# A decoder layer's prompt attention: sparse groups reordered by query tile, values multiplied the other way round, compressed branch once per group, stage ends without store waits

## Chip, cores and metric

One Trainium2 chip, one of its NeuronCores. The metric is the device time of one execution in microseconds (us); lower is better. TensorE (PE) multiplies, VectorE (DVE) and ScalarE (ACT) do elementwise work and reductions, GpSimd (POOL) elementwise work too, SyncE (SP) issues nearly all DMAs. Each engine runs its own instruction stream in order and waits on semaphores.

## What is computed

One layer of a decoder for 512 prompt tokens and 8 sequences of 4 new tokens with 1024 cached ones, in fp32. Cut to what matters here:

```python
proj = rmsnorm(x) @ w_in                      # q, kv, gates, diff q/k/v, merge gates ga, gb
# (A) sparse attention: 16 heads in 4 groups of 4 heads; a group shares its keys and values
s_c = q @ kc.T * scale + bias                 # compressed: 32 blocks of the prompt
s_s = q @ k_sel.T * scale + bias              # selected (for the prompt: all causal keys)
s_w = q @ k_win.T * scale + bias              # sliding window (causal, 512 keys)
o_a = g0*softmax(s_c)@vc + g1*softmax(s_s)@v_sel + g2*softmax(s_w)@v_win
# (B) differential attention: 8 heads, (softmax(s1) - lam*softmax(s2)) @ v, rmsnorm per head
o = sigmoid(ga)*o_a + sigmoid(gb)*o_b
h = x + o @ w_o ;  y = h + relu(rmsnorm(h) @ w_up)**2 @ w_down
```

Outputs are y and the new cache rows.

## The kernel before

The program is five stages, one after the other on all engines: `project` (pj_ tiles), `compress` (cm_), `prompt_attention` (pa_), `decode_attention` (de_) and `finish` (fi_). A stage ends with a barrier over all engines, then its semaphores are cleared and a second barrier stands (`Space.clear`, L95 and L96). At the end of `project`, `compress` and `prompt_attention` SP first waits until the stage's last stores have landed (L418, L826, L1337).

`prompt_attention` walks a list of **units**. First 32 units of the differential heads (`Head`, 8 heads by 4 query tiles t of 128 queries). Then 4 groups of 24 units (`Branch`): for each half hp (two heads of the group) and each query tile t the three branches br 0 (compressed, 32 keys), 1 (selected) and 2 (window), the last two with 128(t+1) keys. A unit does, for its two heads:

- `scores` (PE, L1417): one matmul per head, contraction over 64 rows, the two heads in the two halves of the rows; into bank pair n%2 of `pa_ps_s`.
- `score` (DVE, L1519): adds the bias, writes `pa_sc`, and finds the row maximum (`pa_nmax`).
- `exps` (ACT, L1464): exponential in place, with row sums.
- `turn` (PE, L1430): transposes the probabilities by tiles of 128 into `pa_ps_t`, one bank per head; there are **two banks** for all transposes, used in turn (`TURN_ORDER`, `place`).
- `copy` (ACT L1479 for the first head, DVE L1534 for the second): the turned tiles to `pa_p_t`.
- `values` (PE, L1441): out = P V; the turned probabilities (128 x 128) are the weights and the values (128 x 64) move. fp32 matmuls are two instructions in the trace, transposes one.
- per query tile, after its third unit, `scale_branches` (DVE L1557 to L1559) and `combine_branches` (DVE L1566, L1569), which weigh and add the three branches; POOL then merges with the differential part (L1371, L1372).

Two units are one turn of each engine's loop (j = 0, 2, ...). Transposes and copies are for units j-4 and j-3 (`LAG = 4`). `FILL` says at which j the next head's or group's queries and keys are transposed (`fill`, L1407; copied by ACT L1471 or DVE L1527): a group's at 4 and 2 units before its first unit and 2 after.

SP loads groups 0 and 1 at the start (`load_group`, 12 DMAs each) and group g+2 when all of g is combined. Once the heads are done it also loads for the decode stage: the selected pages, the 8 window pages (`win_load` into `shared.ahead.win`, 256 KB each) and one key page of its first pair of sequences.

In `compress`, DVE at the start fills constants, lays out input half 1 (`lay_out(1)`, L928), then makes the low parts of half 0 (`low_parts`, L951), which TensorE's first large matmul (L1058) waits for.

## Time and profile before

| | |
|---|---|
| time, median of 3 runs | 1687.33 us (1680.7 to 1696.27) |
| profiled execution: time | 1688.51 us |
| profiled execution: span of the instructions | 1686.7 us |
| project / compress / prompt attention / decode attention / finish, by the first instruction of each on PE | 7.5 / 405.2 / 631.1 / 955.3 / 1220 us |
| PE, DVE, ACT busy over the span | 95%, 48%, 34% |
| mean granted TensorE clock | 0.967 of 2.4 GHz |

The span is divided by the stages' starts. PE's busy share is of records whose ends are modelled, so a PE that is always busy isn't a PE at its peak; the distance between starts tells more. The granted clock is 1.00 (2.4 GHz) or 0.50 (1.2 GHz) at any instant.

### The profile page before, as it was taken

The page shows a single profiled execution, that of the slowest core. Times are in us where ns is not written, and L with a number is a line of the kernel's source. Part 1 is how long each engine was busy: PE and PEld are TensorE (multiplying, and loading weights), DVE is VectorE, ACT ScalarE, POOL GpSimd, SP SyncE. Part 2 cuts the span into 40 slices and gives each one's busy share as a digit, 9 for nine tenths or more (in the row PEclk, how much of TensorE's full clock was granted, in tenths as well). Part 3 has the DMA queues.
Part 4 walks back from the last instruction along what each step waited for, and adds up shares of the span by engine and source line. Part 5 has one row for each costly group of instructions (what it writes and reads, how often), then busy time and mean ns, then how long its engine had stood idle before and what let it go on. Part 6 is the DMA issues. An engine that isn't in the chain of part 4 may idle for free. (4 is left out here: it accounts for less than half of the span.)

```text
span 1686.7 us, 31658 instructions
## 1 busy us (share of the span) xinstructions
PE 1603.4 (95%) x12648; PEld 1327.3 (79%) x12648; DVE 801.3 (48%) x1835; ACT 574.1 (34%) x1197; POOL 173.0 (10%) x269
## 2 busy tenths in 40 slices
PE   8999999998999988899899889999899999999998
PEld 5788888875888875667777676666687999999998
DVE  3776633215443418866666545454364442234322
ACT  5323211323322327756555333233333331123210
POOL 1000000000630000084212000000000000000000
PEclk9999999999999998989989799999999999999999
DMA  6445477434631307454121399999742334333421
GB/s 194 155 158 171 164 257 289 153 91 97 188 106 28 107 10 203 99 184 130 34 89 33 112 391 366 368 345 330 279 151 91 125 100 125 100 125 99 125 75 54
DMA packets 185433, 265.67 MB, mean 158 GB/s; under 512 B 35805, under 2 KB 117149, under 8 KB 185190
## 3 DMA queue, kind: packets, MB, share of 16 engines
q1 hardware_dynamic: 174930, 227.31, 41.3%
q0 software_dynamic: 6016, 25.34, 5.0%
q10 hardware_dynamic: 4372, 11.49, 1.8%
q8 instruction: 73, 1.20, 0.3%
q14 instruction: 42, 0.34, 0.1%
HBM read 241.01 MB, written 42.60 MB: 168 GB/s over the span
## 5 line engine op out<-in xcount | busy, mean ns | idle before, releaser
L641 PE MATMUL pj_ps<-all_hi,pj_xh 128*128 128x512 f32 x480 | 192.6, 401 | 0.0
L643 PE MATMUL pj_ps<-all_hi,pj_xl 128*128 128x512 f32 x480 | 190.6, 397 | 0.0
L642 PE MATMUL pj_ps<-all_lo,pj_xh 128*128 128x512 f32 x480 | 190.5, 397 | 0.0
L1464 ACT ACTIVATE pa_sc<-pa_sc,pa_nmax 128x32 f32<-128x32 f32 (+4 forms) x256 | 125.9, 493 | 112.4 <-DVE pa_nmax L1519 111.9
L2763 PE MATMUL fi_ps<-fi_fl,fi_wh 128*128 128x272 f32 x512 | 148.6, 290 | 0.0
L2764 PE MATMUL fi_ps<-fi_th,fi_wl 128*128 128x272 f32 x512 | 148.3, 290 | 0.0
L2762 PE MATMUL fi_ps<-fi_th,fi_wh 128*128 128x272 f32 x512 | 147.6, 288 | 0.7 <-DVE fi_tl L2541 0.7
L2762 PE MATMUL fi_ps<-fi_fh,fi_wh 128*128 128x272 f32 x512 | 147.8, 289 | 0.0
L2764 PE MATMUL fi_ps<-fi_fh,fi_wl 128*128 128x272 f32 x512 | 147.7, 288 | 0.0
L2763 PE MATMUL fi_ps<-fi_tl,fi_wh 128*128 128x272 f32 x512 | 147.2, 287 | 0.0
L2110 ACT ACTIVATE de_slot<-de_ps_t 128x512 f32<-128x512 f32 (+5 forms) x124 | 62.8, 513 | 172.7 <-PE de_ps_t L1944 84.4
L2220 DVE COPY de_slot<-de_ps_t 128x512 f32<-128x512 f32 (+4 forms) x112 | 68.7, 622 | 102.5 <-PE de_ps_t L1944 58.9
L641 PEld LDWEIGHTS pj_ps<-all_hi,pj_xh 128*128 128x128 f32 x480 | 90.7, 189 | 24.6 <-issue 3.4
L643 PEld LDWEIGHTS pj_ps<-all_hi,pj_xl 128*128 128x128 f32 x480 | 90.6, 189 | 21.9
L642 PEld LDWEIGHTS pj_ps<-all_lo,pj_xh 128*128 128x128 f32 x480 | 90.7, 189 | 21.0
L1058 PE MATMUL cm_ph<-cm_xh,all_hi 128*128 128x512 f32 x256 | 103.1, 403 | 2.5 <-DVE cm_xl L951 2.5
L2465 ACT ACTIVATE fi_wh<-all_big 128x2048 fp32r<-128x2048 f32 x30 | 57.3, 1909 | 138.5 <-PE fi_ps L2764 138.5
L1059 PE MATMUL cm_ph<-cm_xl,all_hi 128*128 128x512 f32 x256 | 102.3, 400 | 0.0
L1060 PE MATMUL cm_ph<-cm_xh,all_lo 128*128 128x512 f32 x256 | 102.2, 399 | 0.0
L1430 PE MATMUL pa_ps_t<-all_ident,pa_sc 128*128 128x128 f32 (+1 forms) x464 | 78.4, 288 | 24.1 <-ACT pa_q_t L1471 10.6
L2762 PEld LDWEIGHTS fi_ps<-fi_th,fi_wh 128*128 128x128 f32 x512 | 96.4, 188 | 0.8 <-DVE fi_tl L2541 0.8
L2762 PEld LDWEIGHTS fi_ps<-fi_fh,fi_wh 128*128 128x128 f32 x512 | 96.5, 189 | 0.0
(347 smaller groups left out, 3164.9 us busy)
## 6 DMA issues: line engine op xcount, KB each, us to landing
de_dv<-in_cache_diff SPq DMA_DIRECT2D x64, 512.0 KB, 9.8
all_big<-in_w_in SPq DMA_DIRECT2D x14, 2048.0 KB, 10.6
de_dk<-in_cache_diff SPq DMA_DIRECT2D x48, 512.0 KB, 9.0
all_big<-in_cache_nsa SPq DMA_DIRECT2D x64, 256.0 KB, 6.5
all_big<-in_w_up SPq DMA_DIRECT2D x16, 1024.0 KB, 5.5
all_big<-in_w_down SPq DMA_DIRECT2D x16, 1024.0 KB, 5.7
all_win<-in_cache_win SPq DMA_DIRECT2D x32, 256.0 KB, 7.7
all_dk<-in_cache_diff SPq DMA_DIRECT2D x16, 512.0 KB, 8.5
```

The lines of the kernel that those rows point to most:

```text
L641: pe.matmul(ps[:, t, :], xh[:, k, xk], wh[:, u, k, :], start=k == 0, stop=False)
L642: pe.matmul(ps[:, t, :], xh[:, k, xk], wl[:, u, k, :], start=False, stop=False)
L643: return pe.matmul(ps[:, t, :], xl[:, k, xk], wh[:, u, k, :], start=False, stop=k == KT - 1)
L1058: pe.matmul(o, w1h[k][:, kt, col], mh, start=first, stop=False)
L1059: pe.matmul(o, w1h[k][:, kt, col], ml, start=False, stop=False)
L1060: ins = pe.matmul(o, w1l[k][:, kt, col], mh, start=False, stop=last)
L1430: ins = pe.transpose(bank[0:r, P * k:P * (k + 1)], sc[:, x.n % 6, a, P * k:P * k + r], ident[:])
L1464: nc.scalar.activation(tile, tile, ACT.Exp, scale=-1.0, bias=nmax[:, x.n % 6, a:a + 1], accum_out=x.sums[a]).then_inc(probs, 1)
L2220: ins = nc.vector.tensor_copy(slot[rows, g % 4, cols], ps_t[rows, g % 4, cols])
L2762: pe.matmul(o, hi[:, k, :], a_hi[:, k, tok], start=k == 0, stop=False)
L2763: pe.matmul(o, hi[:, k, :], a_lo[:, k, tok], start=False, stop=False)
L2764: return pe.matmul(o, lo[:, k, :], a_hi[:, k, tok], start=False, stop=k == n_k - 1)
```

## The change

In `prompt_attention`, for the sparse groups only (the heads' units stay):

- A group has 16 units in place of 24 (`NG = 2*QT*2`): selected and window of a query tile, so that one turn of the loop is one query tile.
- The two branches' values are multiplied together (`wide_values`): the values (128 x 64) are the weights, one branch in columns 0 to 63 of the array and one in 64 to 127, and the turned probabilities of both heads (256 columns) move. The result is transposed: ACT copies it (`wide_copy`), PE turns it back (`turn_back`, 2 transposes), DVE combines.
- The compressed branch is done once per group for all 4 heads and 4 tiles: scores (`cs`, 2 fills of 8 matmuls), one maximum, subtraction and exponential over 128 x 512, 4 transposes (`cp`), 4 matmuls with a block-diagonal value matrix (`co`), sums and products on DVE. The next group's transposes and these are put at -10, -8, -6, -4, -2, +4 and +6 units from a group's first unit.
- ACT copies three of four turned blocks (selected of both heads, window of the first), wide results and all key fills; DVE one of four. The order within a turn of ACT's and DVE's loops changes.
- Scratch room is lent from the decode stage's window buffer: 6 of its 8 pages are now loaded in the last group, 2 at the start of the decode stage.
- SP's waits for landed stores go from the ends of the three stages to where the rows are read; in `compress`, `lay_out(1)` comes after the first `low_parts`.

The core of the diff (buffers, semaphores and load lists left out; new PE and DVE parts in full where they are short):

```diff
@@ compress, vector engine
             fill()
-            lay_out(1)
...
                 low_parts(v)
                 if v == 0:
+                    lay_out(1)
                     split()
@@ project / compress / prompt_attention, end of sync engine (each stage alike)
-            for k in range(2):
-                sp.wait_ge(stored[k], 16 * (N_PAIRS + 1))
+            shared.cmp_level = 16 * (N_PAIRS + 1)
@@ prompt_attention
-        NH, NG = DHEADS * QT, 2 * QT * 3
+        NH, NG = DHEADS * QT, 2 * QT * 2
-            FILL[b - 4] = [("q", x, 0), ("k", x, 0)]
-            FILL[b - 2] = [("k", x, 1), ("c", x, 0)]
-            FILL[b + 2] = [("q", x, 1)]
+            for n, more in ((-10, [("q", x, 0)]), (-8, [("k", x, 0)]), (-6, [("k", x, 1), ("c", x, 0)]), (-4, [("q", x, 1)]),
+                            (-2, [("cs", x, 0), ("cs", x, 1)]), (4, [("cp", x, 0)]), (6, [("co", x, 0), ("co", x, 1)])):
+                FILL[b + n] = FILL.get(b + n, []) + more
+        MAX_CMP, EXP_CMP, SUM_CMP = ({first_of(g) + n: g for g in range(GROUPS)} for n in (0, 2, 4))
@@ tensor engine
+            def wide_values(x):
+                pe.wait_ge(combined, x.tile - 1)
+                stand()
+                for unit in (UNITS[x.n - 1], x):
+                    for entry in unit.turns:
+                        pe.wait_ge(*of(entry))
+                        stand()
+                for k in range(x.t + 1):
+                    for unit in (UNITS[x.n - 1], x):
+                        ins = pe.matmul(unit.wide_part, unit.values[k], p_t[:, unit.br, :, P * k:P * (k + 1)],
+                                        start=k == 0, stop=k == x.t)
+                ins.then_inc(wide_done, 1)
+            def turn_back(x):
+                pe.wait_ge(wide_copied, x.m + 1)
+                stand()
+                for a in range(2):
+                    ins = pe.transpose(x.wide[:, a, :], o_t[:, a, :], ident[:])
+                ins.then_inc(valued, 1)
...
                 for x in FILL.get(j, []):
                     fill(x)
+                if NH <= j - LAG - 2 < N:
+                    wide_values(UNITS[j - LAG - 1])
                 for n in (j - LAG, j - LAG + 1):
...
+                if NH <= j - LAG - 2 < N:
+                    turn_back(UNITS[j - LAG - 1])
@@ scalar engine, a turn of the loop within the groups
+                    for x in fills:
+                        fill_copy(x)
+                    if j < N:
+                        exps(UNITS[j])
+                    if NH <= j - LAG - 2:
+                        wide_copy(UNITS[j - LAG - 1])
+                    if j in EXP_CMP:
+                        act.wait_ge(cmp_ready, EXP_CMP[j] + 1)
+                        nc.scalar.activation(cmp_p, cmp_p, ACT.Exp).then_inc(cmp_probs, 1)
+                    for n in (j - LAG, j - LAG + 1):
+                        if n < N:
+                            copy(UNITS[n])
+                    if j < N:
+                        exps(UNITS[j + 1])
@@ vector engine, a turn of the loop within the groups, after score(UNITS[j]), cs / co and score(UNITS[j + 1])
+                    scale_branches(UNITS[j - LAG + 1])
+                    copy(UNITS[j - LAG + 1])
+                if NH <= j - LAG - 2 < N:
+                    combine_branches(UNITS[j - LAG - 1])
+                if j in MAX_CMP:
+                    cmp_most(MAX_CMP[j])
+                if j in SUM_CMP:
+                    cmp_sums(SUM_CMP[j])
@@ combine_branches: 128 x 256 product, then two 128 x 128 sums, in place of 128 x 384 product and reduction
@@ decode_attention, sync engine
             load_new(0)
+            for n in range(6, 8):
+                win_page(sp, d, shared, 0, *divmod(n, WINDOW // P))
...
+            for u in range(2):
+                sp.wait_ge(shared.oa_out[u], 32 * (GROUPS // 2))
```

`cmp_most` is a reduction of 128 x 512 to 128 x 16, a small clamp and a 128 x 512 subtraction; `cmp_sums` a 128 x 512 reduction, a clamp, a reciprocal and 4 small products; `cmp_scores` (cs) adds the bias to 128 x 256 of PSUM, twice; `cmp_outputs` (co) multiplies 128 x 512 of PSUM by coefficients, twice.

## Rows read from the trace of the kernel before

**Rows 1.** The page: busy time of the engines, and the granted clock in 40 slices.
```profile
PE 1603.4 (95%) x12648; PEld 1327.3 (79%) x12648; DVE 801.3 (48%) x1835; ACT 574.1 (34%) x1197; POOL 173.0 (10%) x269
...
PEclk9999999999999998989989799999999999999999
```

**Rows 2.** Stretches: start and end, length, busy per engine, granted clock, DMA share, GB/s.
```profile
762.04:822.01 59.97, 55.06 (x403) 43.91 (x402) 40.53 (x166) 35.09 (x126) 22.19 (x42) 0.91 0.28 82
704.00:882.00 178.00, 162.92 (x1164) 127.38 (x1164) 119.63 (x488) 99.56 (x372) 70.84 (x130) 0.90 0.33 104
882.00:952.00 70.00, 62.84 (x473) 51.21 (x472) 44.65 (x177) 34.30 (x128) 15.36 (x30) 0.92 0.08 24
955.00:1218.00 263.00, 247.31 (x3584) 178.74 (x3584) 122.68 (x345) 84.32 (x165) 11.14 (x20) 0.95 0.96 348
783.30:790.10 6.80, 6.80 (x24) 4.09 (x24) 3.56 (x10) 2.09 (x8) 6.25 (x14) 0.50 0.95 275
796.90:800.40 3.50, 3.32 (x32) 2.98 (x31) 1.63 (x10) 2.56 (x10) 2.06 (x3) 1.00 0.03 11
```

**Rows 3.** Order of time on all engines, one turn of the loop in group 1.
```profile
797.67 0.40 ACT L1464 ACTIVATE pa_sc<-pa_sc,pa_nmax 128x128 f32<-128x128 f32 x1 [1.86 <-DVE pa_nmax L1519]
799.08 1.09 PE L1430 MATMUL pa_ps_t<-all_ident,pa_sc 128*128 128x128 f32 x8 [0.18 <-ACT pa_p_t L1479]
800.01 1.90 PE L1441 MATMUL pa_ps_o<-pa_vs,pa_p_t 128*128 128x64 f32 x16
801.84 0.49 PE L1417 MATMUL pa_ps_s<-pa_keys,pa_q_t 64*128 64x256 f32 x2
```

**Rows 4.** Who waited for whom, 704 to 946 us: total us, times, longest.
```profile
ACT pa_sc L1464 <- DVE pa_nmax L1519: 98.5, 76, 4.6
DVE pa_p_t L1534 <- PE pa_ps_t L1430: 49.4, 66, 1.9
PE pa_ps_t L1430 <- ACT pa_p_t L1479: 9.5, 17, 1.6
```

**Rows 5.** TensorE in order of time in the decode stage (weights of 32 columns).
```profile
1027.11 1.50 PE L2041 MATMUL de_ps_d<-de_dv,de_slot 128*32 128x512 f32 x12
```

**Rows 6.** Groups in group 1 (762 to 822 us), all forms: busy us, mean ns, idle before.
```profile
L1464 ACT ACTIVATE pa_sc<-pa_sc,pa_nmax 128x32 f32<-128x32 f32 (+4 forms) x49 | 23.4, 478 | 23.9 <-DVE pa_nmax L1519 23.8
L1519 DVE CUSTOM_DVE_ANT_0 pa_sc<-pa_ps_s,pa_strip 128x32 f32<-128x32 f32 (+4 forms) x48 | 16.8, 386 | 5.6 <-PE pa_ps_s L1417 5.5
L1534 DVE COPY pa_p_t<-pa_ps_t 32x128 f32<-32x128 f32 (+4 forms) x25 | 10.6, 425 | 12.6 <-PE pa_ps_t L1430 12.5
L1479 ACT ACTIVATE pa_p_t<-pa_ps_t 32x128 f32<-32x128 f32 (+4 forms) x24 | 8.7, 362 | 0.9 <-PE pa_ps_t L1430 0.8
```

**Rows 7.** The same, by form.
```profile
L1464 ACT ACTIVATE pa_sc<-pa_sc,pa_nmax 128x32 f32<-128x32 f32 x16 | 5.0, 314 | 4.8 <-DVE pa_nmax L1519 4.8
L1464 ACT ACTIVATE pa_sc<-pa_sc,pa_nmax 128x512 f32<-128x512 f32 x9 | 6.4, 713 | 9.8 <-DVE pa_nmax L1519 9.8
L1519 DVE CUSTOM_DVE_ANT_0 pa_sc<-pa_ps_s,pa_strip 128x512 f32<-128x512 f32 x8 | 5.2, 682 | 2.8 <-PE pa_ps_s L1417 2.8
L1479 ACT ACTIVATE pa_p_t<-pa_ps_t 128x256 f32<-128x256 f32 x4 | 1.5, 373 | 0.7 <-PE pa_ps_t L1430 0.5
L1566 DVE TENSOR_TENSOR all_late<-pa_ps_o,pa_coef 128x384 f32<-128x384 f32 x8 | 4.4, 552 | 0.1
L1569 DVE TENSOR_REDUCE pa_oa<-all_late 128x128 f32<-128x384 f32 x8 | 4.8, 595 | 0.3
```

**Rows 8.** SP's own waits at the ends of project, compress and prompt attention.
```profile
SPq L418 <- DMA scratch_gb<-pj_y: 1.7, 1, 1.7
...
SPq L826 <- DMA scratch_vc_p<-cm_out: 1.1, 1, 1.1
...
SPq L1337 <- DMA scratch_oa<-pa_oa: 1.9, 1, 1.9
```

**Rows 9.** TensorE at the start of compress, in order of time.
```profile
410.83 0.47 PE L1058 MATMUL cm_ph<-cm_xh,all_hi 128*128 128x512 f32 x1 [2.45 <-DVE cm_xl L951]
```

More of the change, by code:

```diff
@@ L416, in _ @@
             sp.wait_ge(bias_out, 16 * 3)
-            for k in range(3):
-                sp.wait_ge(stored[k], stores[k])
+            shared.rows_level = stores
         @block.scalar
@@ L1174, in prompt_attention @@
         g_in = [s.sem(f"g_in{u}") for u in range(2)]
+        v_in = [s.sem(f"v_in{u}") for u in range(2)]
         h_in = shared.h_in
@@ L1237, in __init__ @@
-                self.clamp = 3e38 if br else 1e29
+                    self.needs += [("k", DHEADS + g, 0), ("k", DHEADS + g, 1)]
+                first, at = P * (QT - 1 - t), 2 * (1 - g % 2)
+                v = (vs, vw)[br]
+                self.lhs = [q_place(g, hp)[x, P * t:P * (t + 1)] for x in HALF]
+                self.width = P * (t + 1)
+                self.rhs = [keys[x, at + br, 0:self.width] for x in HALF]
+                self.values = [v[:, self.u, k, :] for k in range(t + 1)]
@@ L1238, in __init__ @@
+                self.bias = [strip[:, self.u, 2 * hp + x, first:SEQ] for x in range(2)]
+                self.clamp = 3e38
                 self.sums = [rsum[:, self.m % 8, x, br:br + 1] for x in range(2)]
                 self.turns = [("p", n, x) for x in range(2)]
[L1240 to L1242 removed]
+                self.p_t = [p_t[:, br, x, :] for x in range(2)]
@@ L1305, in load_merge @@
                     sp.dma_start(merge[:, k, :, :], tok(d[name][0:SEQ, HPG * DK * g:HPG * DK * (g + 1)])).then_inc(merge_in, 16)
-            load_group(0, 0)
-            load_group(1, 1)
+            for k in range(2):
+                sp.wait_ge(shared.cmp_stored[k], shared.cmp_level)
+            for g in range(2):
+                load_group(g, g)
+                load_values(g, g)
             for h in range(HEADS_AT_ONCE, DHEADS):
@@ L1327, in _ @@
                 if g + 2 < GROUPS:
+                    sp.wait_ge(turned, TURN["q", DHEADS + g, 1] + 1)
+                    load_group(g + 2, g % 2)
                     sp.wait_ge(combined, NH + 2 * QT * (g + 1))
-                    load_group(g + 2, g % 2)
+                    load_values(g + 2, g % 2)
+                if g + 1 == GROUPS:
+                    sp.wait_ge(copied["dve"], copies[TURN["co", DHEADS + g, 1]])
+                    for n in range(6):
+                        win_page(sp, d, shared, 0, *divmod(n, WINDOW // P))
                 for hp in range(2):
@@ L1473, in copy @@
             def copy(x):
-                r = TURN[x.turns[0]]
-                act.wait_ge(turned, r + 1)
-                if x.free_level > 0:
+                if x.n >= NH:
+                    act.wait_ge(*free_level(x))
+                elif x.free_level > 0:
                     act.wait_ge(valued, x.free_level)
-                rows, w = x.values[0].shape[0], P * len(x.values)
-                nc.scalar.activation(x.p_t[0][0:rows, 0:w], ps_t[0:rows, r % 2, 0:w], ACT.Copy).then_inc(copied["act"], 1)
@@ L1481, in _ @@
-            fill_copy(("q", 0, 0))
-            for j in range(0, N + LAG, 2):
-                if j < N:
-                    exps(UNITS[j])
-                for x in FILL.get(j, []):
-                    if copier_of(x) == "act":
-                        fill_copy(x)
+                for a, entry in enumerate(x.turns):
+                    if copier_of(entry) == "act":
+                        r, w = TURN[entry], P * len(x.values)
+                        act.wait_ge(turned, r + 1)
+                        nc.scalar.activation(x.p_t[a][:, 0:w], ps_t[:, r % 2, 0:w], ACT.Copy).then_inc(copied["act"], 1)
```

257 lines of the change are left out of this document (186 added, 71 removed).

## Prediction

> **What bounds the kernel now.** I read the page first: PE is busy 95% of the span, DVE 48%, ACT 34%, and the granted clock is below full mainly in the middle slices [rows 1]. The reader is to see that PE is the busiest engine throughout. Then the stretches: group 1 of the sparse heads takes 59.97 us from its first scores to the next group's, with PE busy 55.1, DVE 40.5 and ACT 35.1 at a granted clock of 0.91; groups 0 to 2 together take 178 us, group 3 with the stage's tail 70 us [rows 2]. Then one turn of the loop in order of time: PE goes from transposes to values to the next scores with a hole of at most 0.2 us (16 value matmuls from 800.01 to 801.84, 0.114 each), while ACT had stood idle 1.86 us before its exponential [rows 3]. The waits say the same: ACT waits 98.5 us for DVE's maxima and DVE 49.4 us for transposes, but PE only 9.5 us for ACT's copies [rows 4]. So PE's program ends last in most turns.
>
> PE's own work in one group, from start-to-start times: values 192 instructions (2 for each of 80 blocks, 32 compressed) x 0.112 = 21.5; transposes 96 x 0.109 = 10.5 (8 take 1.09 us with the last one's tail [rows 3]); scores, whose 512 columns take about 0.43 us per instruction like the decode stage's 512 columns [rows 5], two heads side by side, 8.5, and compressed 2.0; key and query transposes 17 x 0.11 = 1.9. Sum 44.4 of 60.0 us. The other 15.6 are the clock's dips, changes between kinds of matmul (about 0.2 from start to start instead of 0.11: 801.84 less the start of the sixteenth value matmul [rows 3]) and waits for copies.
>
> **The change on PE.** The weights become 64 columns wide and 256 columns move. Bounded by the nearest row: in the decode stage 12 matmuls with weights of 32 columns and 512 moving ones take 1.50 us [rows 5], three rounds of four at 0.43 and a tail; one behind the other they would take 12 x 0.43 = 5.2. So tiles in different columns of the array run side by side. A block of 128 keys of both branches then costs 2 x 0.213 = 0.43, 20 blocks a group: 8.5 us (one behind the other: 17.1). Transposes of probabilities 80 x 0.109 = 8.7; turning back 16 x 0.109 = 1.7; scores 8.5; cs 32 instructions, which within a fill all use the same half of the rows and are bound by their 128 weight columns as the value matmuls are, 3.5; cp 0.4; co 8 x 0.213 = 1.7; other fills 1.9. Sum 35.0, 9.4 less than now.
>
> **ACT and DVE per group.** ACT: exponentials 23.4 less 5.0 for the compressed ones, 18.4; copies of selected and window, half of them, are 8.7 less 8 x 0.25, three of four 10.1 [rows 6, 7]; 8 wide copies x 0.37, one exponential of 128x512 0.7, fills 3.0: 35. DVE: scores 16.8 less 16 x 0.2, 13.6; one copy of four 4.0; coefficients 5; combining 8 x 0.9 (0.55 for 384 columns, so 0.42 for 256, and two sums of 0.2); compressed work 6.3 (0.6 for a reduction of 384 columns, so 0.7 for 512: cmp_most 1.65, cmp_sums 2.0, cs 0.9, co 1.4, the rest small) [rows 6, 7]: 36. All three engines then have about 35 us of work, so none has slack for the others' latency, and I go by the chain of one turn.
>
> **The chain of a turn.** From PE's start of scores: the previous tile's combination, which waits for the turning back, ends on DVE; the first head's score; on ACT two exponentials, the wide copy and two copies; on PE the last transposes (two banks, so the window's second waits for ACT's second copy) and the turning back. For tile t=3, when tile 1 is turned: scores are ready at 1.25; DVE 0.68 and 0.1 to 2.05; exponentials 2 x 0.71 to 3.5; wide copy 0.37 to 3.85; two copies of 0.37 to 4.6 [rows 7]; two transposes to 4.85, turning back to 5.1, next scores at 5.2. In the same way t=0 takes 4.4, t=1 5.2, t=2 4.75; plus 0.2 each for changes of kind. A half of a group is 20.3, a group 40.7.
>
> Extras per group. ACT's fill copy stands ahead of its exponentials and waits for PE's fill, which stands behind two scores: fills delay the chain by 0.35 (-8), 0.65 (-6), 0.55 (-4). The cs fills hold PE and DVE's second score: 2.8. cmp_most delays the next score by 1.65, its exponential 0.7, cp 0.55. At +6 come cmp_sums' 2.0, co through both banks, the next group's first query fill behind them, ACT's copy of it, and only then ACT's exponentials: 4.4 (2.3 in the last group). Sum 11.65. The clock now falls after turns in which PE waits for fills (783.3 to 790.1 at 0.50 [rows 2]); I expect one such dip a group, after cs, at 1.7 us. A group: 54.0 us against 60.0.
>
> **The sum**, against the profiled execution's 1688.51:
> - Groups 0 to 2: 3 x 54.0 = 162 against 178: -16.
> - Group 3 and tail: 40.7 + 5.2 (its own extras) + 1.7 + 13.4 (three turns without scores, combination, POOL, store) = 61 against 70: -9.
> - Heads: group 0's cs and its second query fill come among them: +3.5, between nothing (hidden) and 5.
> - Stage ends: SP waits 1.7, 1.1 and 1.9 us for landed stores [rows 8], all on the path to the barrier: -4.7. The waits reappear ahead of stores and loads that are not needed soon; between -4.7 and -2 if one of them holds something up. In compress the two layouts of about 1.2 us each ahead of the low parts go; PE idles 2.45 us there before its first large matmul [rows 9]: -2.2. DVE splits weights that much later, behind 12 us of matmuls of half 0.
> - Decode: 512 KB more in a stage with DMA at 0.96 and 348 GB/s [rows 2] is 1.5 us if all of it shows, nothing if none: +1. Its key loads are issued 0.9 us later, within this.
> - SP's queue in the stage: load_group(g+2) moves to before group g and load_values to its end; both have most of a group before they are needed, and the stores of oa behind them wait for the same combination as now. POOL starts at the heads' end as before. Nothing.
>
> Sum: -16 - 9 + 3.5 - 6.9 + 1 = -27.4, so 1661; the median of the runs shown is 1.2 below the profiled execution: **1659 us**, this case's own range 1642 to 1675.
>
> One rule of the Trainium skill speaks against the new mixture of matmuls: "TensorEngine Tiling (Array Packing)", Key Properties, says that changing the tiling mode drains the engine. The trace shows 0.2 us instead of 0.11 at such a change [rows 3]. By a full drain, taken as an estimate at 0.27 us each, some 30 changes of a group would cost 8 us instead of 3, and the time would be 10 us more or so where PE ends last.
>
> **Rivals.**
> - *PE-bound as now* (22%): the engines overlap better than my chain says, and a group keeps its ratio of time to PE work, 60.0/44.4 = 1.35: 47.3 us. For: ACT idles 1.86 us before an exponential today and PE doesn't mind [rows 3]. Against: three equal engines. 4 x 12.7 = 51 saved, heads +3.5, ends -6.9, decode +1: 1634.
> - *The saving is eaten* (14%): the two tiles of weights run one behind the other (+5 of the 8.6, the rest in PE's waits), or the turns at +6 and cs cost double. 59 us a group: about 1680, within 1%.
> - *Slower, by the clock* (10%): fewer and wider matmuls with more waiting between them let the clock fall to 0.50 for much of the stage, as it does from 783.3 to 790.1 [rows 2]. At 1.2 GHz PE's 35 us of a group are 70. Against: 796.9 to 800.4, mostly transposes, was at 1.00 [rows 2, 3]. If about three quarters of PE's work run at the low level a group takes 66: 4 x 6 + 3.5 - 6.9 + 1 = +22, 1710. It decides from about 61 us a group, about half of PE's work at the low level. The Trainium skill, "TensorE: Matmul & The Clock Gate", Part 4: PE-mode transpose, has transposes not count as a busy PE for the clock; by that rule this rival would be likely, since transposes are 10.8 of 35 us after and 10.5 of 44 before. The stretch at 1.00 speaks against the rule here.
> - *It does not do what it says* (4%): the groups stay at 60 us and only the stage ends count, about 1683.
>
> **Chances.** Forecast 50%, PE-bound 22%, eaten or ends alone 18%, slower 10%. A measurement of this kernel tells about 1% from no change, so the bounds are 1670.5 and 1704. A little of the forecast's own range lies above 1670.5: faster 0.70, same 0.20, slower 0.10. The range 1626 to 1690 takes in the PE-bound case and the eaten one, and leaves the slow clock out.
>
> **What would show it.** A group's first scores to the next's: 54 us; tiles 4.6 to 5.4 apart, about 8 to 10 at cs and where co and the next query fill meet. Wide matmuls in pairs that start together, pairs 0.21 apart; if the second starts 0.21 later, the tiles don't run side by side. PE's wait for ACT's copies should grow from 9.5 us to several tens. SP's three waits gone, and PE's first large matmul of compress near 407. Clock in the stage 0.90 or above; near 0.6 the slower rival is right. A group under 50 us means that my chain was too long.

## The result, and the profile after

The changed kernel takes 1663.67 us (median; 1659.93 to 1664.96) against 1687.97 of the kernel before: a ratio of 0.9843, 95% interval 0.9808 to 0.9878. (All ratios here are estimated from the single fast runs and can differ a little from the quotient of the medians, here 0.9856.) Predicted were 1659 us, 1642 to 1675 for the leading case, and a range of 1626 to 1690. The profiled execution took 1662.45 us with a span of 1660.6, against 1688.51 and 1686.7.

Where the 26.1 us of the two spans went, by the first instruction of each stage on PE and the first scores of each group:

| part | before | after | difference | term of the prediction |
|---|---|---|---|---|
| start of `project` (7.5 and 8.9) | | | +1.4 | none |
| end of `project` to start of prompt attention | 230.2 | 225.5 | -4.7 | -1.7 - 1.1 - 2.2 = -5.0 |
| heads | 72.9 | 74.7 | +1.8 | +3.5 |
| groups 0, 1, 2 | 178.0 | 162.5 | -15.5 | -16 |
| group 3, tail, end of the stage | 73.3 | 64.6 | -8.7 | -9 - 1.9 = -10.9 |
| decode attention and finish | 731.4 | 731.0 | -0.4 | +1 |

So the sum held nearly term by term; the last group gave about 2 us less than forecast. The sizes inside the terms did not hold as well, and the reason why a turn takes the time that it takes was not the one that I gave. The first sign is in the groups, which the prediction had all alike. The changed kernel by stretches, from a group's first scores to the next group's (the last to the first decode instruction):

```profile
core 0: us, PE busy (x) PEld busy (x) DVE busy (x) ACT busy (x) POOL busy (x), PEclk, DMA share, GB/s
702.49:750.18 47.69, 40.80 (x276) 27.30 (x276) 35.91 (x130) 31.05 (x100) 28.99 (x52) 0.97 0.32 111
750.18:809.83 59.65, 47.68 (x302) 30.14 (x301) 37.13 (x136) 35.77 (x107) 21.91 (x41) 0.90 0.37 107
809.83:864.97 55.14, 48.16 (x303) 30.90 (x302) 36.28 (x135) 33.26 (x104) 19.27 (x36) 0.87 0.29 86
864.97:929.60 64.63, 50.03 (x324) 31.24 (x323) 41.30 (x154) 36.36 (x111) 16.24 (x32) 0.92 0.17 53
```

The first three answer to the group of [rows 2]: 47.7, 59.7 and 55.1 us against 58 to 60, with a mean of 54.2 where the prediction had 54.0. Since the three lie 12 us apart, that their mean agrees so well is luck in part. DVE (36 to 37 us) and ACT (31 to 36) are as busy as its sums of 36 and 35 said. The granted clock, the column behind POOL, runs from 0.97 to 0.87. A clock of 0.87 over 55.14 us is 14.3 us at the low level (the part at 0.50 is twice what is missing to 1.00); the prediction had one dip of 3.4.

Two heads' and two branches' values, from the timeline of PE:

```profile
738.70 0.38 PE L1525 MATMUL pa_ps_o<-pa_p_t,pa_vs 128*64 128x256 f32 x1
738.70 0.38 PE L1525 MATMUL pa_ps_o<-pa_p_t,pa_vw 128*64 128x256 f32 x1
738.91 0.38 PE L1525 MATMUL pa_ps_o<-pa_p_t,pa_vs 128*64 128x256 f32 x1
738.92 0.38 PE L1525 MATMUL pa_ps_o<-pa_p_t,pa_vw 128*64 128x256 f32 x1
```

The first column is the start. Selected (`pa_vs`) and window (`pa_vw`) start together, the next pair 0.21 us later: a block costs 0.43 us for both, as predicted. By the Trainium skill, "TensorEngine Tiling (Array Packing)", Key Properties, a change of tiling mode drains the engine. A step of that kind shows here: from the last pair of this passage (739.99) to the next transpose (740.31) are 0.32 us instead of the 0.21 of a pair. The trace does not tell that a drain is its cause.

From the waits between 705 and 929 us:

```profile
DVE pa_p_t L1712 <- PE pa_ps_t L1513: 54.7, 29, 4.7
PEld pa_ps_t L1513 <- ACT pa_p_t L1597: 32.8, 33, 3.4
ACT pa_sc L1571 <- DVE pa_nmax L1697: 25.1, 16, 3.5
PE pa_ps_t L1513 <- ACT pa_p_t L1597: 24.1, 28, 3.2
```

PE's wait for ACT's copies grew from 9.5 us to 24.1, ACT's for DVE's maxima fell from 98.5 to 25.1 [rows 4]. Two turns of group 2 show who waits for whom where it is worst. DVE, ACT and PE at the turn that begins at 829.20, where the compressed sums and products stand:

```profile
830.35 0.68 DVE L1665 TENSOR_REDUCE pa_cmp_coef<-all_win 128x16 f32<-128x512 f32 x1
831.06 0.47 DVE L1666 TENSOR_SCALAR pa_cmp_coef<-pa_cmp_coef 128x16 f32<-128x16 f32 x1
831.56 0.25 DVE L1667 RECIPROCAL pa_cmp_coef<-pa_cmp_coef 128x16 f32<-128x16 f32 x1
831.85 1.13 DVE L1670 TENSOR_TENSOR pa_cmp_coef<-pa_cmp_coef,pa_gates 128x4 f32<-128x4 f32 x4
833.19 0.69 DVE L1697 CUSTOM_DVE_ANT_0 pa_sc<-pa_ps_s,pa_strip 128x512 f32<-128x512 f32 x1 [0.21 <-PE pa_ps_t L1463]
...
835.85 0.60 ACT L1580 ACTIVATE pa_q_t<-pa_ps_t 128x512 f32<-128x512 f32 x1 [5.41 <-PE pa_ps_t L1490]
...
835.16 0.66 PE L1490 MATMUL pa_ps_t<-all_ident,pa_q 128*128 128x128 f32 x4 [2.05 <-DVE all_win L1679]
```

DVE makes the sums (830.35 to 832.98) while the scores of the tile wait; then come its two scores and the products; PE's query transposes wait for a bank that the products free, and ACT, in order, waits for those transposes ahead of its exponential. That is the turn at +6 that the prediction priced at 4.4 us extra. Behind both long waits of PE in this group the clock falls: this one is followed by 6.8 us at the low level from 835.8, the wait of 2.65 us that ended at 820.97 by 3.4 us from 822.2. Of the eight falls in the four groups ahead of the stage's tail five come with such a wait, of 2.05 to 3.18 us. The other three (at 747.1, 805.1 and 863.1) come with no wait of PE above 0.32 us in the 7 us before; each comes during the 32 small matmuls of the next group's compressed scores or within 1.4 us of the start of their last. The last of the three, with a line for PE and one for the stretch ahead of the fall (columns as above):

```profile
858.78 3.23 PE L1455 MATMUL pa_ps_t<-pa_kc_t,pa_q_t 64*128 64x32 f32 x32
...
856.00:863.12 7.12, 6.80 (x52) 5.04 (x52) 4.05 (x11) 3.86 (x14) 0.91 (x2) 1.00 0.15 39
```

PE is busy for 6.80 of these 7.12 us, and the clock falls at 863.12 all the same. It is the dip after the compressed scores that the prediction expected; those behind the waits it did not. In e_nocmp below, which has no compressed scores, groups 0, 2 and 3 stay at full clock.

### The profile page after: what moved, and what is told of

Its sections match the earlier page's. It is cut to its first block and busy times, and to the rows that moved or that the text cites. A ratio compares the mean times of both kernels' runs of the same rounds, so it can differ in the third digit from the quotient of the medians.

```text
span 1660.6 us, 30744 instructions
## 1 busy us (share of the span) xinstructions
PE 1564.8 (94%) x12248; PEld 1270.9 (77%) x12248; DVE 789.1 (48%) x1723; ACT 576.7 (35%) x1118; POOL 172.4 (10%) x269
## 3 DMA queue, kind: packets, MB, share of 16 engines
q1 hardware_dynamic: 175506, 227.41, 41.9%
## 5 line engine op out<-in xcount | busy, mean ns | idle before, releaser
L1571 ACT ACTIVATE pa_sc<-pa_sc,pa_nmax 128x128 f32<-128x128 f32 (+3 forms) x192 | 105.5, 552 | 38.5 <-DVE pa_nmax L1697 38.3
L1513 PE MATMUL pa_ps_t<-all_ident,pa_sc 128*128 128x128 f32 x400 | 71.1, 304 | 31.0 <-ACT pa_p_t L1597 24.1
```

What stands on the lines that cost most here:

```text
L1513: ins = pe.transpose(bank[0:r, P * k:P * (k + 1)], sc[:, x.n % 6, a, P * k:P * k + r], ident[:])
L1571: nc.scalar.activation(tile, tile, ACT.Exp, scale=-1.0, bias=nmax[:, x.n % 6, a:a + 1], accum_out=x.sums[a]).then_inc(probs, 1)
```

## The experiments

All are one edit of the changed kernel unless said otherwise. On three of the chips used (those of all runs but e_hide, e_serial, e_nocmp and e_ends), PE had gaps in the compress stage that the first chip does not show, and that stage was about 20 us longer (402 to 646 us against 405 to 628), in the kernel before as well by its median: 1709 to 1711 us instead of 1690. So totals are compared by their ratio to the kernel before on the same chip, and the parts by the length of the prompt attention stage on PE (301.8 us in the changed kernel, 324.2 before). Group 2 by its turns, the distances between the first scores of consecutive query tiles, j counted from the group's first unit:

```
j                      0     2     4     6     8     10    12    14    sum   low clock
changed kernel        4.87  7.59  6.91 10.72  5.71  5.97  5.36  8.00   55.1   14.2
e_hide                4.83  6.29  5.36  8.12  4.51  5.97  5.36  8.02   48.5    4.1
e_nocmp               4.82  5.21  4.93  6.07  4.51  5.97  5.36  5.06   41.9    0
e_serial              5.02  7.71  6.27 10.10  4.63  6.45  6.27  8.38   54.8    3.6
e_late                4.16  6.41  5.36  9.56  4.51  5.97  5.36  8.01   49.3    2.0
e_loads               5.69  5.37  5.39  7.35  4.64  5.97  5.45  8.58   48.4    7.5
e_turns               3.51  6.18  6.39  7.59  4.82  6.12  6.39  9.07   50.1    2.9
```

The last column is the time at the low clock level, in us, by the clock records.

**e_hide: are the compressed passages on the path?**

```diff
@@ vector engine, ahead of the copy of the window block instead of behind the combination
                     scale_branches(UNITS[j - LAG + 1])
+                if j in MAX_CMP:
+                    cmp_most(MAX_CMP[j])
+                if j in SUM_CMP:
+                    cmp_sums(SUM_CMP[j])
+                if NH <= j - LAG < N:
                     copy(UNITS[j - LAG + 1])
```

> The changed kernel with VectorE's compressed maxima (about 1.8 us) and compressed sums (2.8 us) moved to just ahead of its copy of a turned block, where it idles about 2 us a turn for PE's transposes. Chain theory (a turn is a chain over PE, DVE and ACT, and both passages stand in it): about 4 us less a group, 2 in the first, 14 to 16 us in all: 1648 against 1663. PE theory (a group's time follows PE's work, the rest is hidden): within 2 us of the changed kernel, 1662 to 1665.

Measured: 1645.33 us, ratio 0.9733 (0.9707 to 0.9758), 1.1% below the changed kernel; stage 281.8 us, 20.0 shorter. The passages are on the path, and the change that put them there can be improved by two moved calls. The chain theory had 14 to 16 us. DVE at the same place now:

```profile
816.67 0.69 DVE L1665 TENSOR_REDUCE pa_cmp_coef<-all_win 128x16 f32<-128x512 f32 x1
817.39 0.17 DVE L1666 TENSOR_SCALAR pa_cmp_coef<-pa_cmp_coef 128x16 f32<-128x16 f32 x1
817.60 0.25 DVE L1667 RECIPROCAL pa_cmp_coef<-pa_cmp_coef 128x16 f32<-128x16 f32 x1
817.89 0.75 DVE L1670 TENSOR_TENSOR pa_cmp_coef<-pa_cmp_coef,pa_gates 128x4 f32<-128x4 f32 x4
818.67 0.29 DVE L1712 COPY pa_p_t<-pa_ps_t 128x128 f32<-128x128 f32 x1
```

There it used to sit idle for PE's transposes. But the gain is more than the passages: the turn at j=8, which holds none, fell from 5.71 to 4.51, because there the clock is full now. The whole group gained 6.7 us, while 10.1 us less were spent at the low level. Over all four groups that time fell from 39.2 to 15.7 us; at 0.4 us each (b_ends below) some 9 of the 20 us are clock, as an estimate. The gain lies in groups 1, 2 and 3 (6.3, 6.7 and 6.8 us); group 0 gained 0.3.

**e_serial: does PE's work decide?**

```diff
-                for k in range(x.t + 1):
-                    for unit in (UNITS[x.n - 1], x):
+                for unit in (UNITS[x.n - 1], x):
+                    for k in range(x.t + 1):
```

> The changed kernel with all selected blocks multiplied before all window blocks, so that the two column tiles no longer run side by side: 0.43 us more for each of 20 blocks of a group, 8.5 us of PE's work a group. PE theory: it all shows, with the group's ratio of time to work even more, 34 us or above in all, 1698. Chain theory: it shows in the turns where the values end later than DVE's score and ACT's exponentials, and is hidden in the turns that score 512 keys and multiply one block; about 5 to 6 us a group, 1684 to 1688. If the pairs don't really run side by side: no change.

Measured: 1670.13 us, ratio 0.989 (0.986 to 0.9919), stage 305.2 us. Neither expectation, and the trace tells why. Four blocks, PE's timeline (a line with x5 holds five that start 0.2 us apart):

```profile
823.95 1.29 PE L1525 MATMUL pa_ps_o<-pa_p_t,pa_vs 128*64 128x256 f32 x5
824.87 0.43 PE L1525 MATMUL pa_ps_o<-pa_p_t,pa_vw 128*64 128x256 f32 x1
825.08 0.38 PE L1525 MATMUL pa_ps_o<-pa_p_t,pa_vs 128*64 128x256 f32 x1
825.13 0.38 PE L1525 MATMUL pa_ps_o<-pa_p_t,pa_vw 128*64 128x256 f32 x1
...
825.56 1.24 PE L1525 MATMUL pa_ps_o<-pa_p_t,pa_vw 128*64 128x256 f32 x5
```

In the program all eight selected instructions (four blocks of two) stand ahead of all window ones. In the trace the first window one starts at 824.87, when three selected ones have yet to start (the fifth of the line with x5 starts at 824.86). With six of each it starts beside the third (845.18 and 845.19 in another turn), with four or two of each beside the first. So the edit did not cost 8.5 us of PE a group but 0, 0, 2 and 4 instructions of 0.21 us in turns of one to four blocks, 2.6 us a group. And just that shows in the turns: j=10 multiplies three blocks and went from 5.97 to 6.45 (0.48, for 0.43 worked out), j=12 four and from 5.36 to 6.27 (0.91, for 0.86). The same two steps stand at j=10 in groups 0 and 3 and at j=12 in all groups; only the turn at j=10 of group 1 did not grow (7.50 and 7.44). In these turns every bit of PE's time shows, at full clock; my count of hidden values was wrong. That alone does not decide between the theories, since the chain theory also let it show where the values end late; e_late does.

In group 2 as a whole the time did not grow (54.8 against 55.1): the group spent 3.6 us at the low clock instead of 14.2. That the added work is what kept the clock up is not shown. Over the stage 3.4 us were added, of 10 worked out.

**e_nocmp: what do the compressed parts cost?**

```diff
-                            (-2, [("cs", x, 0), ("cs", x, 1)]), (4, [("cp", x, 0)]), (6, [("co", x, 0), ("co", x, 1)])):
+                            ):
-        MAX_CMP, EXP_CMP, SUM_CMP = ({first_of(g) + n: g for g in range(GROUPS)} for n in (0, 2, 4))
+        MAX_CMP, EXP_CMP, SUM_CMP = {}, {}, {}
```

> The changed kernel without the compressed branch's scores, maximum, exponential, transposes, products and sums (its part of the output is left out, the same addition is made of another operand). Chain theory: the extras of a group (cs 2.8, maxima 1.65, exponential 0.7, cp 0.55 and most of the 4.4 where the outputs and the next queries meet) and the dip of the clock go, 10 to 11 us a group and 3.5 among the heads, 1617 to 1622. PE theory: only the 5.6 us of PE's work a group at a ratio of 1.35, 7.6 us a group, 1633. If the compressed work is hidden: above 1650.

Two waits that name the compressed work go or move with it. Measured: 1629.37 us, ratio 0.9634 (0.9606 to 0.9662), stage 262.1 us. The first three groups and one wait:

```profile
696.21:735.56 39.35, 33.79 (x233) 21.40 (x232) 32.65 (x119) 29.66 (x99) 23.33 (x40) 1.00 0.38 135
735.56:789.59 54.03, 39.70 (x258) 24.19 (x258) 31.92 (x122) 34.53 (x106) 26.28 (x51) 0.87 0.30 86
789.59:831.52 41.93, 36.60 (x259) 22.28 (x258) 31.26 (x121) 31.57 (x103) 20.60 (x39) 1.00 0.52 154
```

```profile
PE pa_ps_t L1492 <- DMA pa_kc<-scratch_kc_p: 8.7, 1, 8.7
```

Group 2 takes 41.9 us without them, at full clock, 13.2 less than in the changed kernel, and more than either theory had (10 to 11 and 7.6); the prediction's chain without compressed work is 40.7 + 1.55 (the plain fills) = 42.25. Group 1 is another matter: there PE waits 8.7 us for the load of group 2's keys. SP issues it behind its wait for POOL's squares of the heads. (13.7 us at the low clock follow.) The kernel had got ahead of that load, so the total fell by 34 us and not by the 41 to 46 of the chain theory. The heads are 71.3 us long against 74.7: the compressed scores cost 3.4 there.

**e_ends: the stages' ends**

```diff
@@ end of sync engine in project, compress and prompt_attention
+            for k in range(3):
+                sp.wait_ge(stored[k], stores[k])
@@ compress, vector engine
             fill()
+            lay_out(1)
...
                 if v == 0:
-                    lay_out(1)
                     split()
```

> The changed kernel with SP's three waits for landed stores back at the ends of the stages and input half 1 laid out first again in the compress stage. The sum's term for these was 6.9 us (4.7 + 2.2): 1670.5 against 1663.7. Rival: the waits only moved, and the stages' ends are held by something else too: under 3 us, 1664 to 1666.

Measured: 1671.3 us, ratio 0.9891 (0.9868 to 0.9915), about 8 us more than the changed kernel. On PE the gap between project and compress is 1.7 us longer, compress with its end 3.8 (226.8 against 223.0), the end of prompt attention 2.0 (5.8 against 3.8): 7.5 us where the prediction had 6.9. The term is confirmed by the trace; the two totals' intervals overlap.

**b_ends: the same edits in the kernel before** (without the wait at the end of prompt attention, whose room the stage after it reuses).

> The kernel before with only the waits for landed stores moved away from the ends of project and compress, and input half 1 laid out behind the first low parts (the wait at the end of the prompt attention stays). By the prediction's terms 1.7 + 1.1 + 2.2 = 5.0 us less than before, a ratio of 0.997. If the stages' ends and the start of compress are held by something else: 1.000.

Measured: 1697.65 us, ratio 0.9938 (0.9908 to 0.9969). The 5 us are there: in the trace PE's gaps ahead of compress and of prompt attention are 1.8 and 1.2 us shorter than before (2.53 and 2.75 us), and the first large matmul of compress comes 2.1 us sooner after the stage's first. The profiled execution shows something else beside them. Groups 1 and 2, and behind them group 2 of the kernel before:

```profile
772.59:829.47 56.88, 51.97 (x405) 41.80 (x405) 40.24 (x165) 34.96 (x126) 22.19 (x42) 0.97 0.32 99
829.47:885.49 56.02, 50.53 (x406) 41.28 (x405) 39.97 (x164) 32.04 (x123) 12.56 (x24) 1.00 0.31 92
...
822.01:882.00 59.99, 55.19 (x402) 43.25 (x402) 39.80 (x165) 32.21 (x123) 12.55 (x24) 0.91 0.29 86
```

The program of these groups is that of the kernel before, where they take 60.0 us at 0.91 [rows 2]. Here group 2 has a clock of 1.00 and takes 56.0. That is the price of the clock in this kernel, 4.0 us for 10.2 us at the low level, 0.4 us each; groups 0 and 1, compared in the same way, give 0.35 and 0.45. So how often the clock falls hangs on more than what a group does. (It is another chip, and the groups start at other times; which of the two is the cause is not shown.)

**e_two: the share of the copies.** VectorE copies two of four turned blocks as before the change.

```diff
-            return "act" if kind in ("q", "cp") or early or (kind == "p" and half == 0) or sparse else "dve"
+            return "act" if kind in ("q", "cp") or early or (kind == "p" and half == 0) else "dve"
...
+                    copy(UNITS[j - LAG])
                     scale_branches(UNITS[j - LAG + 1])
```

> The changed kernel with VectorE copying the second head's turned block of both branches (two of four) and ScalarE the first head's, as before the change; DVE's added copy stands after its scores and ahead of the coefficients. If the share of three in four is worth what the chain of a turn says: ACT loses about 0.45 us a turn from its chain, but DVE's copy comes only after four scores, so PE's third transpose waits for it instead: within 8 us of 1663.7 on either side, and slower rather than faster (1664 to 1672). If ACT's time alone decided a turn: 32 x 0.45 = 14 us less, 1649.

Measured: ratio 0.9875 (0.984 to 0.9909), stage 302.3 us against 301.8. No difference that can be told, as the first expectation had it: the share of the copies gives nothing measurable by itself in either direction.

**e_qfirst, e_late, e_best, e_loads: what is late after e_hide.** e_qfirst puts the next group's queries ahead of the compressed products:

```diff
-                FILL[b + n] = FILL.get(b + n, []) + more
+                FILL[b + n] = more + FILL.get(b + n, []) if n == -10 else FILL.get(b + n, []) + more
```

> The kernel with the two compressed passages hidden (1645.3), with the next group's query transposes ahead of the compressed products in the turn where both stand. There ACT idled 5.4 us behind its copy of the queries in the changed kernel. Chain theory: the turn of 8.1 us loses 1.5 to 2.5, in three groups: 5 to 7 us less, 1639. If the queries only trade places with the products: 1645.

Measured: ratio 0.975 (0.9721 to 0.9779), stage 284.6 us against 281.8: a miss. The turn at j=6 fell from 8.12 to 6.82 us in groups 0 and 2, as expected, and rose to 12.27 in group 1. PE's waits from 765 to 800:

```profile
PE pa_ps_t L1490 <- DMA pa_kc<-scratch_kc_p: 3.8, 1, 3.8
```

It is the load of e_nocmp again. e_late moves DVE's combination, and also ACT's square root by one turn:

```diff
@@ vector engine: the combination one turn later, between the two scores
                     score(UNITS[j])
+                if NH <= j - LAG - 4 and j <= N:
+                    combine_branches(UNITS[j - LAG - 3])
...
-                if NH <= j - LAG - 2 < N:
+                if j >= N:
                     combine_branches(UNITS[j - LAG - 1])
```

> The kernel with the two compressed passages hidden (1645.3), with VectorE's combination of a query tile (1.0 to 1.3 us) moved one turn later, between the scores of the next tile's two units, so that DVE scores as soon as PE has the scores; ScalarE's square root one turn later too. Chain theory (DVE's queue ahead of its first score is on the chain): 0.6 to 0.9 us a turn, 28 turns, 17 to 25 us less: 1620 to 1628. PE theory: 1645.

Measured: ratio 0.9759 (0.972 to 0.9799), which e_hide's interval overlaps; stage 280.2 us, 1.6 shorter than e_hide's. By groups: 2.8 us less in group 1, where the square root moved, 1.4 less in group 0, and 0.9 and 0.7 more in groups 2 and 3. In group 2 the turns at j=8, 10 and 12 are the same to the hundredth, 4.51, 5.97 and 5.36: DVE's queue was not on their path. In group 0 it was. There POOL works on the heads' results, DVE's two sums of a combination take 0.77 us each instead of 0.29, and PE waits longer for ACT's copy; the turn at j=8 fell from 5.22 to 4.51, that at j=10 from 6.39 to 5.97. The same transposes at j=8, in e_hide and in e_late:

```profile
726.85 0.93 PE L1513 MATMUL pa_ps_t<-all_ident,pa_sc 128*128 128x128 f32 x6 [1.02 <-ACT pa_p_t L1597]
...
747.62 0.93 PE L1513 MATMUL pa_ps_t<-all_ident,pa_sc 128*128 128x128 f32 x6 [0.31 <-ACT pa_p_t L1597]
```

Two of the turns of group 2 in e_late, j=10 and 12:

```profile
848.52:854.49 5.97, 5.66 (x45) 3.93 (x44) 3.37 (x16) 4.45 (x16) 1.83 (x3) 1.00 0.52 178
854.49:859.85 5.36, 5.04 (x36) 2.82 (x35) 4.25 (x16) 3.80 (x15) 3.78 (x8) 1.00 0.00 0
```

PE is busy for 5.66 of 5.97 us, DVE for 3.4, ACT for 4.5. What is left is PE's wait of 0.31 us for ACT's copy of the first transposed block, since there are two banks. e_late and e_serial agree: a turn without compressed work is bound by PE, as long as POOL does not slow DVE down.

e_best is e_hide, e_qfirst and e_late together.

> The hidden compressed passages, the queries ahead of the compressed products, the combination one turn later and the square root one turn later, together. Apart, the second was eaten by ACT's wait for POOL before the square root (its turn took 12.3 us in group 1) and the third gave nothing where PE is busy all the turn. If that reading is right, the turns with products take about 6.8 us in all groups and group 1 has no such wait: 6 to 9 us less than with the passages hidden alone, a ratio to before of 0.968 to 0.970. If the single results add up as measured: 0.976.

Measured: ratio 0.9761 (0.9725 to 0.9796), stage 279.8 us: the lower expectation is refused, since the turn in group 1 still took 11.15 us. e_loads takes the cause away:

```diff
@@ sync engine
-            sp.wait_ge(o_sq, 1)
-            load_merge(0)
             for g in range(GROUPS):
...
                     load_group(g + 2, g % 2)
+                    if g == 0:
+                        sp.wait_ge(o_sq, 1)
+                        load_merge(0)
                     sp.wait_ge(combined
```

> The combined version with SP's loads of group 2's queries and keys ahead of its wait for POOL's squares, instead of behind it. With the queries first, PE stood 3.8 us in group 1 for such a load, and that turn took 11 to 12 us instead of 6.8 in the other groups. If that load is the cause: group 1 falls from 54.7 us to about 48 to 49, 5 to 6 us in all, a ratio to before of 0.972 to 0.973. If the turn is held by something else (POOL, ACT's square root): 0.976 as before.

Measured: 1664.83 us beside 1709.92 of the kernel before, ratio 0.9735 (0.9696 to 0.9773). The turn in group 1 takes 6.82 us (the others 6.82 to 7.35), and group 1 fell from 54.7 to 49.8 us, some 2 of it by 4.9 us less at the low clock (an estimate, at 0.4 each). The stage is 277.4 us, the shortest of all with the full computation, but 2.4 less than e_best's and not 5 to 6, since group 2 took 1.7 us more, with 7.5 us at the low clock instead of 2.5:

```profile
722.80:768.49 45.69, 41.35 (x277) 27.61 (x276) 36.59 (x127) 30.51 (x97) 26.21 (x47) 0.95 0.43 140
768.49:818.25 49.76, 44.59 (x302) 28.78 (x301) 39.14 (x136) 36.30 (x107) 21.81 (x40) 0.95 0.23 72
818.25:866.69 48.44, 45.81 (x302) 29.27 (x301) 37.73 (x135) 33.88 (x104) 22.39 (x43) 0.92 0.46 133
```

So the cause of the long turn is settled. e_hide and e_loads, 0.9733 and 0.9735, are both faster than the changed kernel; the intervals do not tell them apart, nor from e_best's.

**e_between and e_turns: values between the transposes.**

```diff
@@ tensor engine
-                if NH <= j - LAG - 2 < N:
-                    wide_values(UNITS[j - LAG - 1])
                 for n in (j - LAG, j - LAG + 1):
                     if 0 <= n < N:
                         turn(UNITS[n])
...
+                    if n == j - LAG and NH <= n - 2 < N:
+                        wide_values(UNITS[n - 1])
```

> The kernel with the two compressed passages hidden (1645.3), with the wide value matmuls between the transposes of a turn's two units instead of ahead of both, and ScalarE's wide copy between its copies of the two units. Chain theory (ACT's wide copy of 0.37 us stands between its exponentials and the copies that PE's last transposes wait for): 0.3 to 0.4 us a turn, 10 to 12 us less, 1633 to 1635. If the values end after the exponentials, so that they are the longer branch: within 3 us of 1645.

Measured (on top of e_hide): ratio 0.9857 (0.9824 to 0.9889), stage 303.9 us, 22 longer. A new wait leads ACT's from 720 to 940 us:

```profile
ACT pa_p_t L1597 <- PE pa_ps_o L1525: 40.5, 25, 4.1
```

The room for the turned probabilities is single; ACT may copy the next tile only when the values of the last have been multiplied, which is later now. I had left that wait out. e_turns gives the selected half a second room, on top of e_best:

```diff
+                self.p_all = spare_p if br == 0 and self.m % 2 else p_t[:, br, :, :]
...
-            return (wide_done, x.m) if x.m else (valued, NH)
+            m = x.m - 1 + x.br
+            return (wide_done, m) if m > 0 else (valued, NH)
```

> The previous kernel with the wide values between the transposes of a turn's two units again, but now with a second room for the turned selected probabilities, so that ACT's copies of the first unit need not wait for the values of the tile before (one selected page of the decode stage is loaded at that stage's start instead). If that wait of 40 us in all was what made the order slower, it is gone, and PE no longer idles 0.3 us and more a turn for ACT's copy: 8 to 14 us less than the previous kernel, ratio 0.960 to 0.964, less 0.002 if the late page shows in the decode stage. If the order itself is at fault (values after the first unit's transposes end too late for ACT's wide copy): slower than the previous kernel, 0.975 or more.

Measured: ratio 0.9765 (0.973 to 0.9801), stage 283.4 us against 279.8. The wait of 40 us is gone and the order still does not pay. In the turn at j=12 (6.39 us instead of 5.36) PE meets another:

```profile
859.44 0.33 PE L1516 MATMUL pa_ps_t<-all_ident,pa_sc 128*128 128x128 f32 x1 [0.58 <-ACT pa_q_t L1583]
...
862.66 0.41 PE L1536 MATMUL pa_ps_o<-all_ident,all_late 128*128 128x128 f32 x2 [0.20 <-ACT all_late L1589]
```

The second transpose needs the bank of the query fill, which ACT has yet to copy; and at the end the turning back waits for the wide copy. Values ahead of both transposes cover just these two. By the length of the stage the order of the change is the better one; the ratios, 0.9765 and 0.9761, do not tell the two apart.

## Why the prediction was right, step by step

- **The saving of the groups, -16 for three and -9 for the last**: measured -15.5 and about -6.8 (64.6 and the 1.9 of the stage's end taken off against 73.3). Held, with errors that cancel, below. No run takes the wide values, the new order of the units or the single compressed passage out by itself, so what each gave of this saving is not measured.
- **PE's new values, 0.43 us a block for both branches**: held, pairs start together and 0.21 us apart.
- **The chain of one turn, 4.4, 5.2, 4.75 and 5.2 us with 0.2 more each**: without compressed work the turns take 4.82, 5.21, 4.93 and, with a fill, 6.07; then 4.51, 5.97, 5.36 and 5.06. 41.9 us a group, worked out 42.25. The size held, **the reason did not**: "All three engines then have about 35 us of work, so none has slack for the others' latency, and I go by the chain of one turn" is the step that failed. DVE's combination taken out of the way gained nothing in these turns of group 2 (e_late), and 0.43 and 0.86 us of PE's added cost 0.48 and 0.91 (e_serial). PE's own sequence of scores, fills, values and transposes, with one short wait for ACT, is as long as the chain that I had drawn through DVE and ACT, and it is the one that ends last. The turn was right and the engine wrong, and the expectation for e_late, made from the same chain, missed by about 20 us.
- **The extras**: against e_nocmp's turns in group 2 the compressed scores cost 2.9 (8.00 less 5.06) for 2.8 worked out; the maxima with the exponential 2.4 for 2.35; the turn at +4, with the transposes, 2.0 for 0.55; the turn at +6 4.65 for 4.4 less the part of the plain query fill; the turn at +8 1.2 for nothing; among the heads, where group 0's compressed scores stand, 3.4 for 3.5. But the clock is in these differences: 3.3 us at the low level lie in the turn at +4, 4.1 at +6, 2.7 at +8 and 1.9 at +14. At 0.4 us each that explains what is too much at +4 and +8, and leaves about 3.0 at +6 and 2.2 for the compressed scores. So the passages were priced too high, at +6 above all. That DVE's passages end last in these turns is e_hide's finding.
- **The clock, one dip of 1.7 us a group**: too small. Groups 1 and 2 spent 11.9 and 14.2 us at the low level, which at 0.4 us each (b_ends) is 5 to 6 us. The dip at the compressed scores came with three of the four groups' scores; those behind PE's waits of 2 us and more came on top. Of the 13.2 us between group 2 and its bare form some 5.6 are clock and 7.6 the passages themselves, where the prediction had 1.7 and 10.1. The two errors largely cancel, and that is luck.
- **All groups alike**: wrong. Group 0 takes 47.7 us: its first turn is 2.87 us long, since the copies and values beside it are still those of a head, and it had 3.1 us at the low clock. Group 1 takes 59.7: ACT's square root stands at the end of its turn j=6, with two loads of ACT's tables of 1.28 us each, and the turn at j=8 takes 7.45 us. In e_late the root stands one turn later, and with it the long turn: 4.51 at j=8 and 7.43 at j=10. The kernel before has the root too, and there ACT had slack for it (its group 1 takes 60.0, as group 2). I had not asked what lies beside a single event once ACT's slack is gone.
- **SP's queue, nothing**: right for the changed kernel. But group 2's loads stand behind SP's wait for POOL's squares, and kernels that come to them sooner wait for them (3.8 us in e_qfirst, 8.7 in e_nocmp; e_best's long turn went when e_loads moved them). The prediction had the queue in its list and did not give the margin.
- **Stage ends, -6.9**: 7.5 by e_ends; the first large matmul of compress comes 3.5 us after the stage's first instead of 5.6, after an idle 0.73 us instead of 2.45 [rows 9]. It comes at 408.4 where 407 was forecast; the project stage had started 1.4 us later.
- **Heads +3.5, decode +1**: +1.8 and -0.4 in the trace. The heads' own part was 3.4 by e_nocmp; the rest came back there as the heads spent 6.6 us at the low clock instead of 15.6. The decode stage shows no cost for the two later pages.
- **The rivals**: "PE-bound as now" was half right, on the turns without compressed work; its total of 1634 was not reached even with the passages hidden (1645, e_hide). "The saving is eaten" did not come true as to the tiles, and did in part at +6. "Slower, by the clock" did not: the stretches are at 0.87 and above. (This rival's 61 us a group, by its own sum, only bring the kernel back to its old time; the bound of 1704 would take about 65.) By the Trainium skill, "TensorE: Matmul & The Clock Gate", Part 4: PE-mode transpose, transposes don't count as a busy PE; in group 2 of e_nocmp 113 of PE's 259 instructions are transposes and the clock is at 1.00 throughout, so no loss follows from that share here.

## What to carry to other kernels

When a turn of a loop spans three engines, write down the sum of each engine's own sequence beside the chain through the others; where they are within some tenths of each other, as here, the sums did not tell which one ends last; the experiments did, and an edit to the wrong one gained next to nothing. Once-per-group passages belong where their engine idles in every turn, and not where the next tile's work queues behind them: two moved calls were worth 1.1% here, two thirds of what the whole change had given, in part by the clock that they kept up. Ahead of a large saving look for the loads and single events (a table load, a wait for another engine's slow job) that the old pace covered, and give each its margin in us.

## What the runs showed that I had not expected

- Matmuls in different column halves of the array do not keep the program's order of starts: with eight of one half queued ahead of eight of the other, the ninth of the program started beside the fifth (824.87 and 824.86). The Trainium skill, "TensorE: Matmul & The Clock Gate", Part 3: Packing small matmuls, has matmuls in strict order by start and end; the starts in this trace differ from that, and so do the lengths of the turns, which grew by the part that did not overlap and no more. With two or four instructions of each half the halves overlapped in full without interleaving; with six and eight they did not.
- A low clock cost about 0.4 us per us (60.0 against 56.0 us for the same program, on two chips), less than the 0.5 of an engine that does nothing but multiply at half the rate. On one chip the turn at j=8 of group 2 gives the same: 5.71 us with 2.7 us at the low level, 4.51 with none (e_hide), 0.44 each.
- An elementwise instruction on DVE took up to 2.7 times as long while POOL worked. The addition at L1753 in e_hide took 0.78 us beside POOL's products from 723.34 on, 0.57 at 807.42 beside POOL's from 806.98 to 807.84, and 0.29 by itself:

```profile
723.44 0.78 DVE L1753 TENSOR_TENSOR all_late<-all_late 128x128 f32<-128x128 f32 x1
...
813.62 0.29 DVE L1753 TENSOR_TENSOR all_late<-all_late 128x128 f32<-128x128 f32 x1
```

- On three chips PE had gaps in the first 100 us of compress that the profile puts down to no releaser; the stage was some 20 us longer in every profile taken there. I did not look for their cause.
